# The last head's prompt state leaves the mixer and is multiplied in the routing pause, from copies in DRAM

## The chip, the cores and the metric

The kernel runs on one core of a Trainium2 chip. The metric is the device time of one execution in microseconds; the median of the timed runs counts. TensorE is called PE below, VectorE DVE, ScalarE ACT, GpSimd POOL and SyncE SP.

## What is computed

One layer of a hybrid decoder over 272 prompt positions (16 learned ones and 256 given) and 8 sampled tokens. A mixer (a projection of the normed input, a causal convolution of width 31 and a four-head retention) is followed by a mixture of 16 experts. Cut to what the change touches:

```python
def _retention_chunk(q, k, v, S, lg):
    ...
    k_dec = k * jnp.exp((L - 1.0 - idx)[:, None] * lg[None, :])[None, :, :, None]
    S_new = jnp.exp(L * lg)[None, :, None, None] * S + jnp.einsum('bjhd,bjhe->bhde', k_dec, v)
    return o, S_new
# mixer
y_a = jax.nn.silu(cn).astype(h.dtype) @ w_conv_out
y_b = (on * jax.nn.silu(g_ret.astype(jnp.float32))).astype(h.dtype) @ w_ret_out
out = (g_a * y_a + g_b * y_b) @ w_o
# experts, for t = the normed rows
eid = g_sel[:, None] * EXPERTS_PER_GROUP + idx
comb = p_g[:, None] * jnp.sum(w[..., None] * jax.nn.one_hot(eid, N_EXPERTS, dtype=jnp.float32), axis=1)
act = jax.nn.silu(hg) * hu * comb[:, :, None].astype(hg.dtype)
```

The prompt starts from a zero state, so each head's new prompt state is one product of its decayed keys (272 x 256) and its values (272 x 512), and it is only an output: nothing later in the layer reads it. The sampled tokens have states of their own, 32 of 256 x 512 (4 heads by 8 sequences), which are read, updated and written.

## The kernel before

**Mixer.** The projections and output products are 112 units (`UNITS`, numbered w); each makes 128 output features for up to 280 tokens, from 8 blocks of 128 inputs. Weights are float32 and every product is made in three passes: ACT makes the high part of a unit's weights (`hi`, w_hi), DVE the remainder (`lo`, w_lo), PE multiplies high by high, high by low and low by high (`passes`). Weights come in 1 MB chunks for two units each into three raw buffers. SP issues a load as soon as the last reader of its buffer (`lo`) is done. `hi` and `lo` of unit w + 2 are issued at the head of iteration w.

The retention runs beside the units, 22 steps from unit 37 (`STEP0`); k = w - STEP0. For each head h, step 4h has ACT and DVE write the decayed keys (k_tok, k_two), and step 4h + 4 makes the head's prompt state (tiles S, L1841 and L1842): for each of its two halves two float32 products of 512 columns and one single-pass one. ACT copies them to S_out (L920), and POOL stores them. The sampled states go through seven slots: POOL loads one, ACT scales it (`scaled`, L805), DVE adds the new outer product (L1323), PE multiplies by the queries (`samp_o`, L1788), POOL stores it; a slot's next load waits for the store to land. At the end of a head ACT copies the samples' sums out of their bank (osb, L948), and PE brings them to features one step later (tile ot, L1900). DMAs of states are on POOL's queue, weights on SP's.

The first unit of the convolution's output (cout) and of the last product (wo) read operands that ACT and DVE make one block after another; PE waits for each block with the semaphores clo_ready and mlo_ready.

**Routing pause.** After unit 111 PE brings the rows back to tokens (`to_tokens`). Then DVE chooses experts for every token in some forty small steps, while PE waits; four float32 products that nobody reads (`turn_over(4)`, L1756) stand in that wait. Then come the positions (tile pos), the rows of the first expert (tiles xp, L1959), the list of rows (idx, L1969) and the slot weights (tile ws, `weigh`, L1979).

**Experts.** 96 chunks of 1 MB are streamed through rings of four split chunks (`stream`, L2018: 12 products of 512 columns each); the name is g, u or d with the expert's number. On DVE the slot weights' copy (`slot_weights`, L1533) comes ahead of the remainders of chunks 2 and 3, of the tile Q (`last_slots`), which PE transposes in `last_places` behind chunks 0 and 1, and of what follows.

PE writes banks of PSUM in the order of the list `TILES`, seven in rotation; to open one it waits until the tile seven places ahead in the list was copied out.

## Time and profile before

| | us |
|---|---|
| median of 3 runs (lowest, highest) | 767.28 (767.08, 767.32) |
| the profiled execution's own time | 767.98 |
| its span | 766.2 |
| PE busy, DVE busy, ACT busy | 747.7, 667.9, 515.5 |

### The profile page before, as it was taken

The page shows a single profiled execution, that of the slowest core. Times are in us where ns is not written, and L with a number is a line of the kernel's source. Part 1 is how long each engine was busy: PE and PEld are TensorE (multiplying, and loading weights), DVE is VectorE, ACT ScalarE, POOL GpSimd, SP SyncE. Part 2 cuts the span into 40 slices and gives each one's busy share as a digit, 9 for nine tenths or more (in the row PEclk, how much of TensorE's full clock was granted, in tenths as well). Part 3 has the DMA queues.
Part 4 walks back from the last instruction along what each step waited for, and adds up shares of the span by engine and source line. Part 5 has one row for each costly group of instructions (what it writes and reads, how often), then busy time and mean ns, then how long its engine had stood idle before and what let it go on. Part 6 is the DMA issues. An engine that isn't in the chain of part 4 may idle for free.

```text
span 766.2 us, 12172 instructions
## 1 busy us (share of the span) xinstructions
PE 747.7 (98%) x4755; PEld 656.7 (86%) x4755; DVE 667.9 (87%) x917; ACT 515.5 (67%) x650; POOL 95.5 (12%) x119
## 2 busy tenths in 40 slices
PE   8999999999999999999999999999999999999994
PEld 5999999877777799999999978888888888888873
DVE  5699999888888887999979687988999899998897
ACT  6434446786868774335694465788888888888863
POOL 1100001224333400000020001011111111110000
PEclk9999999999999999999999999999999999999997
DMA  8945446698889954455458475899999999999972
GB/s 347 365 144 191 172 166 247 218 329 306 289 298 331 369 204 167 166 185 201 165 201 306 196 277 205 335 368 370 370 368 362 360 381 376 359 369 345 369 270 79
DMA packets 39030, 213.12 MB, mean 278 GB/s; under 512 B 7275, under 2 KB 7531, under 8 KB 19100
## 3 DMA queue, kind: packets, MB, share of 16 engines
q1 hardware_dynamic: 23268, 165.39, 58.3%
q0 software_dynamic: 15264, 45.55, 16.6%
q10 hardware_dynamic: 432, 1.31, 0.5%
q8 instruction: 40, 0.66, 0.3%
q14 instruction: 26, 0.21, 0.1%
HBM read 192.92 MB, written 31.65 MB: 293 GB/s over the span
## 4 chain that ended last, share of the span: by engine, by line
PE 58%; DVE 19%; DMA 13%; ACT 4%; issue 3%; POOL 1%; SPq 0%; DVEq 0%; ACTq 0%; POOLq 0%
PE bank L2018 34%; PE bank L1711 10%; DVE conv L1180 6%; DVE w_lo L1125 5%; PE bank L1714 5%; DMA out_ret_sample<-S_ring 5%; DMA out_ret_sample<-S_five 3%; DMA out_ret_sample<-xT 3%; DMA raw<-weights 3%; PE bank L2008 2%; ACT w_hi L776 1%; DMA xT<-in_state_ret 1%; PE bank L2050 1%; PE bank L1959 1%; DVE rot L1229 1%
## 5 line engine op out<-in xcount | busy, mean ns | idle before, releaser
L1130 DVE TENSOR_TENSOR ring_lo<-raw,ring_hi 128x2048 fp32r<-128x2048 f32 x72 | 163.5, 2288 | 22.5 <-ACT ring_hi L783 22.5
L1711 PE MATMUL bank<-h_hi,w_hi 128*128 128x264 f32 (+1 forms) x632 | 164.4, 292 | 0.3 <-ACT oT L941 0.3
L1711 PE MATMUL bank<-h_lo,w_hi 128*128 128x264 f32 (+1 forms) x632 | 161.4, 288 | 0.0
L1125 DVE TENSOR_TENSOR w_lo<-raw,w_hi 128x1024 fp32r<-128x1024 f32 x112 | 136.6, 1220 | 26.9 <-ACT w_hi L776 26.5
L776 ACT ACTIVATE w_hi<-raw 128x1024 fp32r<-128x1024 f32 x112 | 117.9, 1052 | 55.4 <-PE bank L1714 51.0
L783 ACT ACTIVATE ring_hi<-raw 128x2048 fp32r<-128x2048 f32 x72 | 138.2, 1919 | 20.0 <-PE bank L2018 19.1
L1711 PEld LDWEIGHTS bank<-h_hi,w_hi 128*128 128x128 f32 x632 | 119.1, 188 | 2.2 <-issue 1.5
L1711 PEld LDWEIGHTS bank<-h_lo,w_hi 128*128 128x128 f32 x632 | 119.1, 188 | 0.6
L1180 DVE SCALAR_TENSOR_TENSOR conv<-u,vec,conv 128x256 f32<-128x256 f32 x240 | 101.7, 477 | 0.6
L1714 PE MATMUL bank<-h_hi,w_lo 128*128 128x264 f32 (+1 forms) x632 | 92.3, 289 | 0.2 <-DVE w_lo L1125 0.2
L1714 PEld LDWEIGHTS bank<-h_hi,w_lo 128*128 128x128 f32 x632 | 84.5, 188 | 0.4 <-DVE w_lo L1125 0.4
L2018 PE MATMUL bank<-ring_hi,x_hi 128*128 128x512 f32 x192 | 76.2, 397 | 0.0
L2018 PE MATMUL bank<-ring_lo,x_hi 128*128 128x512 f32 x192 | 75.5, 393 | 0.0
L2018 PE MATMUL bank<-ring_hi,x_lo 128*128 128x512 f32 x192 | 75.5, 393 | 0.0
L1130 DVE TENSOR_TENSOR w_lo<-raw,w_hi 128x2048 fp32r<-128x2048 f32 x24 | 54.9, 2287 | 5.6 <-ACT w_hi L783 4.9
L783 ACT ACTIVATE w_hi<-raw 128x2048 fp32r<-128x2048 f32 x24 | 46.0, 1916 | 5.5 <-PE bank L2018 2.8
L2018 PEld LDWEIGHTS bank<-ring_lo,x_hi 128*128 128x128 f32 x192 | 36.5, 190 | 7.8
L2018 PEld LDWEIGHTS bank<-ring_hi,x_lo 128*128 128x128 f32 x192 | 36.4, 190 | 7.4
L2018 PEld LDWEIGHTS bank<-ring_hi,x_hi 128*128 128x128 f32 x192 | 36.4, 190 | 7.4
L733 POOL DMA_INDIRECT y_rows<-Y,idx x14 | 21.5, 1536 | 160.4 <-ACT Y L1087 160.4
L2018 PE MATMUL bank<-ring_hi,aT_lo 128*128 128x512 f32 x96 | 37.4, 389 | 0.0
L2018 PE MATMUL bank<-ring_lo,aT_hi 128*128 128x512 f32 x96 | 37.4, 389 | 0.0
(325 smaller groups left out, 1418.8 us busy)
## 6 DMA issues: line engine op xcount, KB each, us to landing
raw<-weights SPq DMA_DIRECT2D x152, 1024.0 KB, 7.0
S_ring<-in_state_ret POOLq DMA_DIRECT2D x20, 512.0 KB, 7.1
out_ret_sample<-S_ring POOLq DMA_DIRECT2D x20, 512.0 KB, 6.7
xT<-in_state_ret POOLq DMA_DIRECT2D x8, 512.0 KB, 6.9
out_ret_sample<-xT POOLq DMA_DIRECT2D x8, 512.0 KB, 7.3
S_five<-in_state_ret POOLq DMA_DIRECT2D x4, 512.0 KB, 5.4
out_ret_sample<-S_five POOLq DMA_DIRECT2D x4, 512.0 KB, 10.1
out_ret_prompt<-S_out POOLq DMA_DIRECT2D x8, 256.0 KB, 6.6
```

The costliest lines, as they stand in the source:

```text
L733: pool.indirect_dma_start(YD, bass.IndirectOffsetOnAxis(ap=idx[:, NE + e:NE + e + 1], axis=0), Y[:, e % 2, :], None, bounds_check=2 * N - ...
L776: act.activation(part_view(w_hi, w), raw_view(w), ACT.Copy).then_inc(hi_ready, 1)
L783: act.activation(ring_view(ring_hi, k), raw[raw_slot(c)][:, :].rearrange("p (k n) -> p k n", k=4), ACT.Copy).then_inc(chunk_hi, 1)
L1125: dve.tensor_tensor(part_view(w_lo, w), raw_view(w), part_view(w_hi, w).bitcast(f32), ALU.subtract).then_inc(lo_ready, 1)
L1130: dve.tensor_tensor(ring_view(ring_lo, k), raw[raw_slot(NCM + k)][:, :].rearrange("p (k n) -> p k n", k=4), ring_view(ring_hi, k).bitcast( ...
L1180: dve.scalar_tensor_tensor(out=out, in0=src, scalar=w_t, in1=out, op0=ALU.mult, op1=ALU.add).then_inc(conv_step, 1)
L1229: link(dve.tensor_tensor(rot[:, 1, :, cols], qk[:, p % 2, :, cols], sin2[:, :, cols], ALU.mult))
L1711: pe.matmul(out, hi[:, k, cols], b[:, k0 + k, :], start=first and k == 0 and j == 0, stop=False)
L1714: ins = pe.matmul(out, lo[:, k, cols], x_hi[:, k0 + k, :], start=False, stop=last and k == ks - 1)
L1959: ins = pe.matmul(b[:, f * 128:(f + 1) * 128], h2[0:nt, tt, at_f:at_f + 128], sel0[0:nt, tt, :], start=tt == 0 and f == 0, stop=tt == 2 an ...
L2008: ins = pe.transpose(b[:, f * 128:(f + 1) * 128], xg[:, e % 2, at_f:at_f + 128], ident)
L2018: ins = pe.matmul(out, a[:, kk, :], b[:, kk, :], start=first and kk == 0 and j == 0, stop=last and kk == 3 and j == 2)
```

## The change

- The state product of head 3 (`LATE`) is no longer made at step 16. Instead SP copies head 3's values and keys (v, v_two, k_tok, k_two: 512, 160, 256 and 80 KB) to DRAM (`late_to_dram`) ahead of weight chunk 29, and back into other places of SBUF (`late_back`) ahead of chunk 45. PE makes the same two products from them in the routing pause (`late_state`), ACT copies the result, SP stores it. The four products that nobody reads become one.
- The copies take the place, in SBUF, of the ring's fourth chunk, so ACT's split of chunk 3 waits for the stores. ACT and DVE wait for the copies to DRAM before they write over the sources.
- The other steps and the convolution's shares per unit stay where they were.
- `weigh(0)` is put between the two chunks of the first expert's g. Its bank is opened where it was. DVE's order is what it was.
- The first unit of cout and of wo takes the three passes of a block together, where before all low-weight passes stood at the end.

```diff
+LATE = NH - 1
@@ TILES
-            if 4 <= k <= 16 and k % 4 == 0:
+            if 4 <= k <= 16 and k % 4 == 0 and k // 4 - 1 != LATE:
                 for dt in range(2):
                     add((("S", k // 4 - 1, dt), "A"))
...
     add((("lg", 1), "D"))
+    for dt in range(2):
+        add((("S", LATE, dt), "A"))
@@ sync
+            def late_to_dram():
+                evacuated(sp, ("vt", 4 * LATE + 3))
+                sp.dma_start(V_SP, v_tok[LATE][:, 0:2, :]).then_inc(late_out, 16)
+                sp.wait_ge(vhi_ready, 2 * LATE + 2)
+                sp.wait_ge(vlo_ready, LATE + 1)
+                sp.dma_start(V2_SP, v_two[:, LATE % 2, :].bitcast(f32)).then_inc(late_out, 16)
+                evacuated(sp, ("kt", LATE, 0))
+                evacuated(sp, ("kt", LATE, 1))
+                sp.dma_start(K_SP, k_tok[:, :, :]).then_inc(late_out, 16)
+                sp.dma_start(K2_SP, k_two[:, :].bitcast(f32)).then_inc(late_out, 16)
+            def late_back():
+                seen(sp, ("m", FIRST["gate_b"] - 1))
+                sp.wait_ge(rows_stored, 16 * 3)
+                sp.wait_ge(late_out, 16 * 4)
...
             for c in range(NCM + RS + 2):
+                if c == (STEP0 + 14 + 7) // 2:
+                    late_to_dram()
+                if c == (FIRST["gate_b"] + 4 + 7) // 2:
+                    late_back()
                 load_weights(c)
...
+            for dt in range(2):
+                evacuated(sp, ("S", LATE, dt))
+                sp.dma_start(O["ret_prompt"][0, 0, LATE, dt * 128:(dt + 1) * 128, :], v_late[:, dt, :]).then_inc(late_stored, 16)
@@ scalar
+                if k == 3:
+                    act.wait_ge(late_stored, 16 * 2)
...
+            seen(act, ("S", LATE, 1))
+            for dt in range(2):
+                free(act.activation(v_late[:, dt, :], bank(("S", LATE, dt))[:, :], ACT.Copy))
@@ tensor, passes
+                if w in (FIRST["cout"], FIRST["wo"]):
+                    pe.wait_ge(lo_ready, w + 1)
+                    for k in range(ks):
+                        pe.wait_ge(clo_ready if w == FIRST["cout"] else mlo_ready, k + 1)
+                        for j, (a, b) in enumerate(((hi, x_hi), (hi, x_lo), (lo, x_hi))):
+                            ins = pe.matmul(out, a[:, k, cols], b[:, k, :], start=k == 0 and j == 0, stop=k == ks - 1 and j == 2)
+                    return ins
@@ tensor, pause
+            def late_state(dt):
+                pe.wait_ge(late_in, 16 * 4)
+                b = opened(("S", LATE, dt))
+                for tt in range(2):
+                    pe.matmul(b[:, :], k_late[:, tt, dt * 128:(dt + 1) * 128], v_late[:, tt, :], start=tt == 0, stop=False)
+                done(pe.matmul(b[:, :], k_late_two[:, dt * 128:(dt + 1) * 128], v_late_two[:, :], start=False, stop=True))
             to_tokens(1)
-            turn_over(4)
+            late_state(0)
+            late_state(1)
+            turn_over(1)
@@ tensor, experts
-                weigh(rd)
+                slots = opened(("ws", rd))
                 if rd:
+                    weigh(rd, slots)
...
                             if i == 1 and e == 0 and not rd:
+                                weigh(rd, slots)
                                 evacuated(pe, ("xp", e, 1, rd))
```

On SP's queue, from the first weight loads to the stores of the normed rows (raw<-weights is a weight chunk, h_rows<-h the rows), this stood before:

```order
L607 DMA x_tok<-tokens 128x1024
L619 DMA raw<-weights 128x2048 x63
L624 DMA h_rows<-h 128x1024 x2
L624 DMA h_rows<-h 8x1024
L619 DMA raw<-weights 128x2048 x89
```

and this stands there now:

```order
L630 DMA raw<-weights 128x2048 x29
L634 DMA v_later<-v 128x1024
L637 DMA v_two_later<-v_two 80x512
L640 DMA k_later<-k_tok 128x512
L641 DMA k_two_later<-k_two 80x256
L630 DMA raw<-weights 128x2048 x16
L648 DMA v_late<-v_later 128x1024
L649 DMA k_late<-k_later 128x512
...
L630 DMA raw<-weights 128x2048 x18
L661 DMA h_rows<-h 128x1024 x2
L661 DMA h_rows<-h 8x1024
L664 DMA out_ret_prompt<-v_late 128x512 x2
```

Ten DMAs are new on SP: four copies out behind chunk 28, four back behind chunk 44, and head 3's two stores, which were on POOL's queue.

On PE, from the router's products (wrg, xT) through the routing pause to the first expert's g chunks (ring_hi, x_hi), this stood before (L1756 is `turn_over`, VW the slot weights):

```order
L1773 MATMUL bank<-wrg,xT 8x20 x4
L1756 MATMUL bank<-con 128x512 x4
L1944 MATMUL bank<-member,count_r 128x16 x3
L1944 MATMUL bank<-member,count_r 8x16 x3
L1946 MATMUL bank<-member,count_r 128x16 x3
L1756 MATMUL bank<-con 128x512
L1959 MATMUL bank<-Q,h 128x128 x12
L1969 MATMUL bank<-V_,A_ 128x32 x6
L1979 MATMUL bank<-VW,A_ 128x32 x6
L2018 MATMUL bank<-ring_hi,x_hi 128x512
```

and this now:

```order
L1823 MATMUL bank<-wrg,xT 8x20 x4
L1989 MATMUL bank<-v_late,k_late 128x512 x2
L1990 MATMUL bank<-v_late_two,k_late_two 128x512
...
L1806 MATMUL bank<-con 128x512
L2004 MATMUL bank<-member,count_r 128x16 x3
...
L2019 MATMUL bank<-Q,h 128x128 x12
L2029 MATMUL bank<-V_,A_ 128x32 x6
...
L2077 MATMUL bank<-ring_hi,x_hi 128x512
L2077 MATMUL bank<-ring_hi,x_lo 128x512
L2077 MATMUL bank<-ring_lo,x_hi 128x512
L2038 MATMUL bank<-VW,A_ 128x32 x6
```

The two state products (the pair of rows L1989 and L1990 stands twice) replace three of the four unread ones, and the slot weights' six products have moved behind the twelve of the first g chunk.

At the end of cout's first unit PE had this before (c_hi and c_lo are the convolution's blocks):

```order
L1711 MATMUL bank<-c_lo,w_hi 128x264
L1711 MATMUL bank<-c_hi,w_hi 128x264
L1711 MATMUL bank<-c_lo,w_hi 128x264
L1714 MATMUL bank<-c_hi,w_lo 128x264 x8
L1711 MATMUL bank<-c_hi,w_hi 128x264
```

and has this now:

```order
L1757 MATMUL bank<-c_hi,w_lo 128x264
L1757 MATMUL bank<-c_hi,w_hi 128x264
L1757 MATMUL bank<-c_lo,w_hi 128x264
L1757 MATMUL bank<-c_hi,w_lo 128x264
L1761 MATMUL bank<-c_hi,w_hi 128x264
```

Behind the last block's two high-weight passes eight low-weight ones stood; now one does. The first unit of wo reads the same with m_hi and m_lo.

## Rows read from the trace of the kernel before

**Rows 1.** The page's busy times, whole span

```profile
PE 747.7 (98%) x4755; PEld 656.7 (86%) x4755; DVE 667.9 (87%) x917; ACT 515.5 (67%) x650; POOL 95.5 (12%) x119
```

**Rows 2.** The chain that ended last: start, length, what

```profile
233.55 7.70 DMA xT<-in_state_ret
...
241.27 1.06 ACT xT L805
...
258.61 1.72 PE bank L1841 x4
260.32 0.24 PE bank L1842
...
262.51 0.97 PE bank L1788 x8
263.49 2.17 PE bank L1711 x16
...
266.64 0.79 PE bank L1900 x8
...
486.18 16.38 PE bank L2018 x72
```

**Rows 3.** ACT's timeline: start, length, instruction [idle before, releaser]

```profile
256.81 1.06 ACT L805 ACTIVATE S_ring<-S_ring 128x1024 f32<-128x1024 f32 x1 [1.09 <-DMA S_ring<-in_state_ret]
257.88 1.28 ACT L966 ACT_TABLE_LOAD   x1
...
262.83 1.08 ACT L920 ACTIVATE S_out<-bank 128x512 f32<-128x512 f32 x2
263.78 2.38 ACT L948 ACTIVATE osb<-bank 8x512 f32<-8x512 f32 x4
```

**Rows 4.** Busy time by stretch; the last three: clock, DMA share, GB/s

```profile
240.00:250.00 10.00, 9.65 (x67) 7.30 (x64) 9.37 (x16) 6.68 (x12) 3.56 (x5) 1.00 0.89 299
250.00:260.00 10.00, 10.00 (x66) 7.85 (x64) 8.54 (x15) 7.04 (x10) 4.66 (x8) 1.00 1.02 413
```

**Rows 5.** PE's timeline in the first units of cout and wo

```profile
396.40 0.39 PE L1711 MATMUL bank<-c_hi,w_hi 128*128 128x264 f32 x1 [1.42 <-DVE c_lo L1380]
...
397.09 1.13 PE L1714 MATMUL bank<-c_hi,w_lo 128*128 128x264 f32 x8
...
421.10 0.39 PE L1711 MATMUL bank<-m_hi,w_hi 128*128 128x264 f32 x1 [0.65 <-DVE m_lo L1210]
```

**Rows 6.** PE's timeline from the routing pause on

```profile
450.14 3.70 PE L1756 MATMUL bank<-con 128*128 128x512 f32 x8
454.46 0.65 PE L1944 MATMUL bank<-member,count_r 128*128 128x16 f32 x6 [0.62 <-DVE member L1462]
...
463.35 1.52 PE L1979 MATMUL bank<-VW,A_ 128*128 128x32 f32 x12
...
471.87 1.06 PE L1989 MATMUL bank<-con,Q 128*128 128x128 f32 x6
```

**Rows 7.** DVE's timeline from the slot weights to Q

```profile
464.91 0.19 DVE L1533 COPY wslot<-bank 128x32 f32<-128x32 f32 x1
465.83 2.29 DVE L1130 TENSOR_TENSOR w_lo<-raw,w_hi 128x2048 fp32r<-128x2048 f32 x1 [0.72 <-issue]
468.04 2.28 DVE L1130 TENSOR_TENSOR ring_lo<-raw,ring_hi 128x2048 fp32r<-128x2048 f32 x1
470.24 0.95 DVE L1550 TENSOR_TENSOR Q<-mcon,pl 128x768 f32<-128x768 f32 x1
```

**Rows 8.** Busy time by stretch, columns as in rows 4

```profile
464.00:466.00 2.00, 2.00 (x12) 1.70 (x12) 1.06 (x3) 1.85 (x2) 0.56 (x1) 0.73 0.51 121
466.00:468.00 2.00, 2.00 (x6) 1.61 (x5) 2.00 (x1) 0.00 (x0) 0.00 (x0) 0.50 0.37 141
468.00:470.00 2.00, 2.00 (x9) 1.61 (x9) 2.00 (x2) 0.61 (x1) 0.00 (x0) 0.92 0.45 78
...
755.00:766.00 11.00, 0.82 (x4) 0.34 (x2) 7.21 (x12) 4.72 (x11) 0.00 (x0) 0.66 0.28 104
```

More of the change, by code:

```diff
@@ L323, with build @@
     _last[SLOT[_w]] = _w
-def build(nc, A, W, L, H2, YD, C, C2, O):
+def build(nc, A, W, L, H2, YD, LATER, C, C2, O):
     f32, f32r = mybir.dt.float32, mybir.dt.float32r
@@ L432, in build @@
             h2 = me.enter_context(nc.sbuf_tensor("h2", [128, 3, D], f32))
+        with ExitStack() as me:
+            me.enter_context(nc.sbuf_tensor("over_late", [128, 2 * hs // 4], f32))
+            v_late = me.enter_context(nc.sbuf_tensor("v_late", [128, 2, DV], f32))
+            k_late = me.enter_context(nc.sbuf_tensor("k_late", [128, 2, DK], f32))
+            v_late_two = me.enter_context(nc.sbuf_tensor("v_late_two", [80, DV], f32r))
+            k_late_two = me.enter_context(nc.sbuf_tensor("k_late_two", [80, DK], f32r))
+        V_SP, K_SP, V2_SP, K2_SP = LATER
         YY_CHUNKS = (NCE - 5, NCE - 4, NCE - 3)
@@ L482, in build @@
         Sp_stored = [sem(f"Sp_stored{i}") for i in range(2)]
+        late_out, late_in, late_stored = sem("late_out"), sem("late_in"), sem("late_stored")
         rows_stored, y_stored = sem("rows_stored"), sem("y_stored")
@@ L619, in load_weights @@
                 sp.dma_start(raw[raw_slot(c)][:, :], src).then_inc(raw_in[raw_slot(c)], 16)
+            def late_to_dram():
[12 more added lines that the diff above has]
+                sp.wait_ge(late_out, 16 * 4)
+                sp.dma_start(v_late[:, :, :], V_SP).then_inc(late_in, 16)
+                sp.dma_start(k_late[:, :, :], K_SP).then_inc(late_in, 16)
+                sp.dma_start(v_late_two[:, :].bitcast(f32), V2_SP).then_inc(late_in, 16)
+                sp.dma_start(k_late_two[:, :].bitcast(f32), K2_SP).then_inc(late_in, 16)
             for c in range(NCM + RS + 2):
+                if c == (STEP0 + 14 + 7) // 2:
+                    late_to_dram()
+                if c == (FIRST["gate_b"] + 4 + 7) // 2:
+                    late_back()
                 load_weights(c)
@@ L655, in _ @@
             for i in range(2):
-                sp.wait_ge(Sp_stored[i], 16 * NH)
+                sp.wait_ge(Sp_stored[i], 16 * (NH - 1))
+            sp.wait_ge(late_stored, 16 * 2)
         @block.gpsimd
@@ L697, in _ @@
                     load(n - 1 + SLOTS)
-            store_prompt(NH - 1)
             for i in (5, 6):
@@ L849, in _ @@
                     if f == 7:
-                        seen(act, ("S", NH - 1, 1))
+                        act.wait_ge(late_out, 16 * 4)
                     if f == 8:
@@ L913, in _ @@
                         scaled(2 * k + 1)
-                    if 4 <= k <= 16 and k % 4 == 0:
+                    if 4 <= k <= 16 and k % 4 == 0 and k // 4 - 1 != LATE:
                         h = k // 4 - 1
@@ L969, in _ @@
                         if q == 0:
-                            act.wait_ge(Sp_stored[0], 16 * NH)
-                            act.wait_ge(Sp_stored[1], 16 * NH)
+                            act.wait_ge(Sp_stored[0], 16 * (NH - 1))
+                            act.wait_ge(Sp_stored[1], 16 * (NH - 1))
                         seen(act, ("ut", q))
@@ L1213, in _ @@
                     dve.wait_ge(yhi_ready, f + 1)
+                    if f == 5:
+                        dve.wait_ge(late_out, 16 * 4)
                     dve.tensor_tensor(on_lo[:, f, OUT], oT[:, f, OUT], on_hi[:, f, OUT].bitcast(f32), ALU.subtract).then_inc(ylo_ready, 1)
@@ L1704, in passes @@
                 cols = slice(0, 128) if m is None else slice(m * 128, (m + 1) * 128)
+                if w in (FIRST["cout"], FIRST["wo"]):
[5 more added lines that the diff above has]
+                    return ins
                 for k in range(ks):
-                    if w == FIRST["cout"]:
-                        pe.wait_ge(clo_ready, k + 1)
-                    if w == FIRST["wo"]:
-                        pe.wait_ge(mlo_ready, k + 1)
                     for j, b in enumerate((x_hi, x_lo)):
@@ L1831, in _ @@
                     k = w - STEP0
-                    if 4 <= k <= 16 and k % 4 == 0:
+                    if 4 <= k <= 16 and k % 4 == 0 and k // 4 - 1 != LATE:
                         h = k // 4 - 1
@@ L1971, in find, with weigh @@
                 done(ins)
-            def weigh(rd):
+            def weigh(rd, b):
                 pe.wait_ge(vw_ready, 1)
-                b = opened(("ws", rd))
                 for c in range(2):
@@ L2129 @@
     YD = nc.dram_tensor("y_rows", (2 * N, D), _mybir.dt.float32).ap()
-    build(nc, A, W, L, H2, YD, C, C2, O)
+    LATER = (nc.dram_tensor("v_later", (128, 2, DV), _mybir.dt.float32).ap(), nc.dram_tensor("k_later", (128, 2, DK), _mybir.dt.float32).ap(),
+             nc.dram_tensor("v_two_later", (80, DV), _mybir.dt.float32).ap(), nc.dram_tensor("k_two_later", (80, DK), _mybir.dt.float32).ap())
+    build(nc, A, W, L, H2, YD, LATER, C, C2, O)
     r = _run(nc, [arrays], core_ids=[0])
```

## Prediction

> **What bounds the kernel now.** I read the page first, then the chain of work that ended last, then the timelines at the places that the change touches. PE is busy for 98% of the span [rows 1], and from 242 us on the chain consists mostly of PE's own work, one instruction behind the other [rows 2]. So work taken from PE is worth its length only up to the next thing that PE must wait for, and each place has to be read for what stands just behind it. Three such places matter.
>
> The first is the end of the retention. Up to 241 us the chain runs through the transfers of the sampled states: a load of 7.70 us, then ACT's scaling at 241.27, and only then PE [rows 2]. The last state's load is late as well: ACT idles 1.09 us for it and scales at 256.81. From there ACT works without a break: a table load, and at the end the two copies of the prompt state (262.83, 1.08 us) and the copies of the samples' sums, which end at 263.78 + 2.38 = 266.16 [rows 3]. PE needs those sums for the tile ot, which stands in the chain at 266.64 [rows 2]. ACT is thus some 0.4 us from being the bound there.
>
> The second is the first unit of cout and of wo, where PE idles 1.42 and 0.65 us for the last blocks of DVE [rows 5]. The third is the routing pause. PE idles only 0.62 us there beyond the unread products, until DVE has the choice at 454.46 [rows 6]. Behind the slot weights PE is dense until the tile Q is transposed at 471.87. DVE ends Q at 470.24 + 0.95 = 471.19, having worked without a break since 465.83 [rows 7]. DVE is 0.7 us ahead of PE there, no more. In the experts PE is dense: 72 products take 16.38 us, 0.2275 us each [rows 2], and a loss ahead of them is not made good.
>
> **The state product, out of the mixer.** It is four float32 products and two single-pass ones, 2 x (1.72 + 0.24) = 3.92 us of PE from 258.61 on [rows 2]. If PE alone decided, all of it would be gained. But behind it stand the samples' products (0.97 us), a unit from 263.49 on, and then the tile ot, which waits for ACT's copies. ACT's chain from 256.81 loses only the two copies, 1.08 us (less an overlap of 0.1): it ends at 265.1 where it ended at 266.16. The tile ot then starts at some 265.25 in place of 266.5, so the gain is 1.2 us, and 2.7 of the 3.92 us turn into a wait of PE before ot.
>
> **The copies to DRAM.** They are 1008 KB on SP's queue, 1.03 MB. SP can issue them once head 3's keys and values are split, at about 233 to 237 us, behind the weights of chunk 28, so they move at about 240 to 245. From 250 to 260 the DMA engines are fully busy at 413 GB/s, and from 240 to 250 they are busy 0.89 of the time [rows 4]. At 390 GB/s, between the two stretches' rates while busy (299 / 0.89 = 336 and 413), 1.03 MB take 2.65 us. The idle share of 240 to 250 can hide 1.1 us and, with the edges, I take 1.35; the other 1.3 us push the last state's load, for which ACT already waits. The bounds are 0 (SP's copies get in only where POOL's queue is idle) and 2.65. So this stretch nets -1.2 + 1.3 = +0.1 us, between -1.2 and +1.45. On the way back the copies are read in a stretch with half-idle engines, behind which weights are three chunks ahead: 0.
> The Trainium skill speaks against the copies too (page "Trainium Kernel Development and Optimization", section "Key Constraints"): DMAs issued from SP, ACT and POOL all run on the same 16 engines and interleave. A separate queue for the copies would then protect nothing, which is my reading of the full stretch; were it wrong, this stretch would give -1.2.
>
> **The two reordered units.** In cout, behind the last block's arrival at about 396.75, the eight low-weight passes from 397.09 on are 1.13 us by their record, some 0.98 without the overlap, 0.122 each [rows 5]. Seven of them move into the wait ahead, 7 x 0.122 = 0.85 us. But wo's first unit is released by DVE's last block at 421.10 whatever PE did before: DVE is itself dense up to it. The gain of cout is therefore spent as a longer wait before wo, and wo's own 0.85 us is what stays: -0.87 with the pass that is spared a restart. The bounds are 0 (none) and -1.7 (both).
>
> **The routing pause.** The new work is 3.92 + one unread product. The four unread ones take 3.70 us by record, 3.44 from start to start, so one is 0.86 and the new sum 4.78. From 450.2 it ends at 454.98, and the positions could start at 454.46 [rows 6]: +0.5 us, as DVE's next steps wait for them. ACT's two copies fit into its idle time before the first rows, and the stores of 512 KB have about 6 us until ACT's split of chunk 3, at 463.95 before, with idle DMA engines: 0. If they took longer than that, the price would appear one for one on ACT, and DVE's remainder of chunk 3 at 468.04 would be next.
>
> **The slot weights.** This edit moves no work, but it moves who waits. DVE's copy of the slot weights starts at 464.91, just as PE ends them (463.35 + 1.52), and stands ahead of the remainders of chunks 2 and 3 and of Q. From that copy to the end of Q are 471.19 - 464.91 = 6.28 us [rows 7]. Behind the change PE makes the first chunk's 12 products before them: 12 x 0.2275 = 2.73 us. So Q ends 2.73 us later, at 473.92 on the old scale, and PE starts its transpose at 474.0 where it did at 471.87 [rows 6]: +2.1 us. PE has nothing else to do then; it is through with both chunks at 463.42 + 2.73 + 1.46 + 2.73 = 470.3 and idles 3.7 us. Ahead of the change the same stretch of PE was slow for another reason (next part), which DVE's chain hid, so nothing is regained.
>
> **The clock.** After the thin products PE's granted clock was half (1.2 in place of 2.4 GHz): 0.73, 0.50 and 0.92 in three stretches of 2 us make 3.4 us at half clock from 464.9 to 468.3 [rows 8], a loss of 1.7 us of PE's work. At the end of the kernel, where PE is idle, it is 0.66. An idle time of 3.7 us in front of Q should bring such a phase, with dense products behind it that nothing hides: +1.5 us, from 0 to 1.7.
> The Trainium skill agrees in kind (page "TensorE: Matmul & The Clock Gate", section "Why this matters for your kernels"): gaps between bursts of products let the clock fall to half. By that rule this cost is there whenever the wait before Q is; by the trace it is likely.
>
> **The sum.** +0.1 - 0.87 + 0.5 + 2.1 + 1.5 = +3.3 us. On the profiled execution's own time, 767.98 (span 766.2, 1.78 around it), that is 771.3. That execution is 0.7 us above the median of the runs, so against the median of 767.28 I forecast **770.6 us**, 0.43% slower. A measurement of this kernel tells about 0.2%, 1.5 us, from no change.
>
> **Rivals.**
> - *PE decides everywhere, and the mixer pays in full* (12%). The 3.92 us would be gained if ACT could reach its copies earlier than its rows suggest. Then 767.28 - 3.92 - 0.87 + 0.5 + 2.1 = 765.1, faster. For it: the chain from 258.61 to 266.64 is all PE. Against it: ACT's end at 266.16. It decides if PE's ot starts before 264.5 on the old scale.
> - *The wait before Q is there, but the clock holds and the copies are hidden* (14%): 767.28 - 1.2 - 0.87 + 0.5 + 2.1 = 767.8, no difference that can be told. For it: the pause and the first chunk are denser than before.
> - *The copies cost in full, and the half clock falls on the first chunk and again behind the wait* (8%): +1.45 - 0.87 + 0.5 + 2.1 + 1.7 for one phase, and up to 1.7 for the other, which here delays the slot weights too: 773.9.
> - *All new work is hidden, with no wait before Q* (4%): only if DVE's split of chunk 2 got ahead of the slot weights' copy, which its order excludes: 763.7.
>
> The forecast's own case has 62%, from 769 to 772.6. The range to hold 8 in 10 takes in the second rival and ends below the third: 767.4 to 772.8. Faster by over 0.2% has 0.14 (first and fourth, less a part that ends within), within 0.2% 0.14, slower 0.72.
>
> **What the changed profile would show.** Right: idle time of PE of 1 to 3 us before ot, released by ACT's osb; ACT's wait for the last state's load longer than 1.09 us; PE's waits in cout and wo moved ahead, with three products behind the last block; no wait of PE for member; a wait of over 3 us for Q, and a granted clock near 0.5 behind it. The prediction is wrong if PE does not idle for Q, if ot moves forward by 3 us or more, or if ACT's split of chunk 3 waits for the stores (then it is worse).

## The result, and the profile after

| | before | changed |
|---|---|---|
| median (lowest, highest), us | 767.09 (766.41, 768.42), 14 runs | 769.37 (767.99, 773.92), 14 runs |
| ratio, 95% interval | | 1.0036 [1.0026, 1.0046] |
| profiled execution, its span | 767.98, 766.2 | 771.79, 770.0 |

The change makes the kernel 0.36% slower, some 2.8 us (the medians are 2.3 apart); 3.3 were forecast. It also makes it uneven: the runs of before lie within 2 us, those of the changed kernel within 6. Late runs of before exist too, but are few: of 35 more, timed beside e5 to e9, three are above 768, up to 770.10. The profiled execution of the changed kernel is the second longest of its 14, and its mean granted clock, 0.988, is the lowest (the 14 range to 0.994), so it shows more half clock than most runs had. The same kernel timed again gave 769.15 (767.78 to 774.88, 11 runs), 1.0031 [1.0015, 1.0046].

PE's waits in the changed kernel, as the view of waits lists them, longest sum first (sum, times, longest, us). They answer to [rows 5, 6]:

```profile
PE bank L2048 <- DVE Q L1597: 3.5, 1, 3.5
...
PE bank L1950 <- ACT osb L990: 0.9, 1, 0.9
PE bank L1757 <- DVE c_lo L1427: 0.6, 1, 0.6
PE bank L1757 <- DVE m_lo L1255: 0.5, 1, 0.5
```

The wait for c_lo has gone from 1.42 to 0.6, that for member is gone, and two are new: 0.9 before ot (L1950) and 3.5 before Q is transposed (L2048). PE's timeline shows the pause and the wait for Q:

```profile
448.72 1.98 PE L1989 MATMUL bank<-v_late,k_late 128*128 128x512 f32 x4
450.14 0.80 PE L1990 MATMUL bank<-v_late_two,k_late_two 80*128 80x512 f32 x1
450.78 1.88 PE L1989 MATMUL bank<-v_late,k_late 128*128 128x512 f32 x4
452.10 0.80 PE L1990 MATMUL bank<-v_late_two,k_late_two 80*128 80x512 f32 x1
...
465.23 1.42 PE L2038 MATMUL bank<-VW,A_ 128*128 128x32 f32 x12
...
473.03 1.71 PE L2048 MATMUL bank<-con,Q 128*128 128x128 f32 x6 [3.53 <-DVE Q L1597]
```

DVE's timeline tells why Q is late; it answers to [rows 7]:

```profile
466.69 0.19 DVE L1580 COPY wslot<-bank 128x32 f32<-128x32 f32 x1 [2.88 <-PE bank L2038]
467.61 2.29 DVE L1175 TENSOR_TENSOR w_lo<-raw,w_hi 128x2048 fp32r<-128x2048 f32 x1 [0.72 <-ACT ring_hi L825]
469.82 2.28 DVE L1175 TENSOR_TENSOR ring_lo<-raw,ring_hi 128x2048 fp32r<-128x2048 f32 x1
472.02 0.95 DVE L1597 TENSOR_TENSOR Q<-mcon,pl 128x768 f32<-128x768 f32 x1
```

DVE stands idle for 2.88 us in front of a copy of 0.19 us, and the 6.28 us from that copy to the end of Q are the same as before. What the clock does behind the wait, by stretches (the column before the last two is the granted clock), columns as in rows 4:

```profile
468.00:470.00 2.00, 1.50 (x7) 0.90 (x5) 2.00 (x2) 0.46 (x1) 0.00 (x0) 1.00 0.00 0
470.00:472.00 2.00, 0.00 (x0) 0.00 (x0) 2.00 (x1) 0.23 (x1) 0.00 (x0) 0.90 0.43 94
472.00:474.00 2.00, 0.97 (x4) 0.62 (x5) 2.00 (x3) 0.00 (x0) 0.00 (x0) 0.50 1.03 422
474.00:476.00 2.00, 2.00 (x9) 1.65 (x10) 1.85 (x3) 0.18 (x1) 0.00 (x0) 0.50 1.00 356
476.00:478.00 2.00, 2.00 (x7) 1.71 (x7) 1.38 (x2) 1.74 (x3) 0.59 (x1) 0.50 0.98 397
478.00:480.00 2.00, 2.00 (x9) 1.63 (x9) 0.89 (x1) 1.08 (x1) 0.40 (x1) 0.89 0.91 313
```

The clock falls at 471.6, while PE still idles, and is at 1.2 GHz until 478.4 (0.90 and 0.89 of 2 us are 0.4 us each at half, with 6 us between them): 6.8 us, twice the phase of [rows 8], and PE has work in the last 5.4 of them. The length is not fixed. In the second profile of the same kernel (e9), where PE waits for Q until 477.00, the phase behind a wait of 3.52 us is 3.4 us long:

```profile
476.00:478.00 2.00, 1.00 (x6) 0.64 (x6) 2.00 (x3) 0.00 (x0) 0.00 (x0) 0.95 1.04 438
478.00:480.00 2.00, 2.00 (x10) 1.98 (x11) 1.95 (x4) 0.60 (x1) 0.00 (x0) 0.50 0.97 406
480.00:482.00 2.00, 2.00 (x8) 1.57 (x7) 1.26 (x2) 1.90 (x2) 0.99 (x1) 0.69 1.02 377
```

In the mixer there is a second such phase, behind the new wait for ot. ACT's and PE's timelines there, and the clock by stretches:

```profile
255.97 1.06 ACT L847 ACTIVATE S_ring<-S_ring 128x1024 f32<-128x1024 f32 x1 [0.81 <-DMA S_ring<-in_state_ret]
...
261.99 2.38 ACT L990 ACTIVATE osb<-bank 8x512 f32<-8x512 f32 x4
```

```profile
264.42 1.06 PE L1950 MATMUL bank<-con,osb 128*128 128x8 f32 x8 [0.95 <-ACT osb L990]
```

```profile
266.00:268.00 2.00, 2.00 (x14) 2.00 (x13) 2.00 (x5) 1.67 (x5) 0.00 (x0) 0.70 0.86 323
268.00:270.00 2.00, 2.00 (x10) 1.91 (x9) 1.68 (x3) 0.40 (x2) 0.00 (x0) 0.50 0.76 311
270.00:272.00 2.00, 2.00 (x11) 1.76 (x10) 0.61 (x2) 0.26 (x1) 0.00 (x0) 0.94 0.74 233
```

Worked out in the same way, this phase is 3.4 us long. It begins at 266.8, 2.4 us after the wait has ended, while PE is at work.

To compare kernels, the table below gives PE's start times at fixed places of their profiled executions, and stretches between them. "ot" is the tile of [rows 2] at 266.64, whose first product starts at 266.48 before; "gate" is the sum of squares that follows it; "cout" and "wo" are those units' first products, "rows home" the first transpose behind wo, "weights" the first product of what follows the first expert's rows, "Q" its transpose, "down" the first transpose of the first expert's features.

| kernel | ot | ot to gate | cout to wo | wo to rows home | weights to Q | Q to down | span |
|---|---|---|---|---|---|---|---|
| before | 266.48 | 8.53 | 25.23 | 15.57 | 8.52 | 12.83 | 766.2 |
| changed | 264.42 | 10.19 | 24.38 | 15.40 | 10.65 | 15.23 | 770.0 |
| changed, second profile | 268.91 | 10.19 | 24.36 | 14.90 | 10.66 | 14.44 | 773.1 |
| products back (e1) | 264.34 | 8.69 | 24.38 | 14.90 | 7.89 | 12.92 | 762.6 |
| products moved alone (e2) | 265.90 | 8.53 | 25.19 | 15.67 | 10.65 | 15.69 | 770.6 |
| two units alone (e3) | 265.75 | 8.53 | 24.36 | 14.90 | 8.54 | 12.83 | 763.9 |
| wait filled (e4) | 268.35 | 8.68 | 24.36 | 15.26 | 10.64 | 12.89 | 769.5 |
| copies alone (e5) | 265.83 | 8.53 | 25.18 | 15.46 | 8.54 | 12.84 | 765.4 |
| state alone (e6) | 263.85 | 8.67 | 25.20 | 15.14 | 7.90 | 12.89 | 763.3 |
| cout alone (e7) | 266.17 | 8.52 | 24.38 | 15.75 | 8.52 | 12.83 | 765.3 |
| slot copy behind Q (e8) | 264.14 | 8.68 | 24.37 | 14.91 | 7.08 | 12.89 | 761.6 |
| the same, no copies out (e10) | 265.27 | 10.18 | 24.39 | 15.57 | 7.07 | 12.90 | 765.0 |
| the same again (e12) | 263.40 | 8.74 | 24.37 | 15.90 | 7.07 | 12.89 | 762.0 |
| units, products, slot copy (e11) | 266.09 | 8.53 | 24.37 | 14.92 | 7.08 | 12.89 | 762.9 |

### The profile page after: what moved, and what is told of

The parts are those of the page before. It is cut to its first block, busy times and chain, and to the rows that moved or that the text cites. A ratio compares the mean times of both kernels' runs of the same rounds, so it can differ in the third digit from the quotient of the medians.

```text
span 770.0 us, 12172 instructions
## 1 busy us (share of the span) xinstructions
PE 748.5 (97%) x4749; PEld 657.8 (85%) x4749; DVE 668.2 (87%) x917; ACT 515.3 (67%) x650; POOL 94.7 (12%) x117
## 4 chain that ended last, share of the span: by engine, by line
PE 55%; DVE 19%; DMA 15%; ACT 5%; issue 4%; POOL 1%; DVEq 0%; ACTq 0%; POOLq 0%
PE bank L2077 34%; PE bank L1761 9%; DMA out_ret_sample<-S_ring 7%; DVE conv L1225 6%; DVE w_lo L1170 5%; PE bank L1764 5%; DMA out_ret_sample<-xT 3%; DMA out_ret_sample<-S_five 2%; PE bank L2067 2%; DMA raw<-weights 1%; ACT w_hi L816 1%; DMA S_ring<-in_state_ret 1%; PE bank L2111 1%; PE bank L2019 1%; DVE ring_lo L1175 1%
## 5 line engine op out<-in xcount | busy, mean ns | idle before, releaser
L2077 PE MATMUL bank<-ring_hi,aT_hi 128*128 128x512 f32 x96 | 37.3, 389 | 0.0
```

Source lines behind the costliest of these rows:

```text
L2077: ins = pe.matmul(out, a[:, kk, :], b[:, kk, :], start=first and kk == 0 and j == 0, stop=last and kk == 3 and j == 2)
```

## Experiments

The theory was the prediction's: the slot weights' new place makes Q late (2.1) and drops the clock (1.5), the units give 0.87, and the mixer nets nothing. The rivals: the copies to DRAM are the cost; the clock falls for another reason than the wait.

### Which part costs: the slot-weight products

**e1, the products back ahead of the first chunk**, all else as changed:

```diff
-                            if i == 1 and e == 0 and not rd:
-                                weigh(rd, slots)
```
(and `weigh` again behind the first expert's rows.)

> The changed kernel with the slot weights' products back ahead of the first expert's g chunks; state product, copies and the two units as changed. Theory A (the slot weights' place costs 2.1 us of waiting before Q and 2.4 us of half clock behind it): no wait of PE before Q, 766.1 us, 1.0 us faster than before and 3.3 faster than the changed kernel, since at the first rows of the pause the changed kernel was 0.97 us ahead. Theory B (the copies, the state product in the pause or its stores cost the time): as the changed kernel, 769.4 us.

764.94 (763.83 to 770.26, 12 runs), 0.9985 [0.9970, 0.9999]. That is 0.5% from the changed kernel's 1.0036, so the products' place costs 3.9 us (uncertain by 1.4; the stretches of the two profiles give 2.76 + 2.31 = 5.1). The clock stays at 1.00 through the pause, and of the wait for Q 0.8 is left:

```profile
PE bank L1950 <- ACT osb L990: 1.3, 1, 1.3
...
PE bank L2048 <- DVE Q L1597: 0.8, 1, 0.8
```

"Weights to Q" is 7.89, less than the 8.52 of before, although the order there is the same: before had half clock on the first chunk, and this kernel, with the state product in the pause, has not. e6 shows the same (7.90). The prediction had no term for it.

**e2, the kernel before with only the products moved.**

> The kernel before with only the slot weights' products moved between the two g chunks. Theory A: PE idles 3 to 3.7 us before Q, the clock is half behind it, 767.1 + 2.1 + 2.4 = 771.6 us (range 769.5 to 772). Theory B: 767.1 us, no change. A third theory, that the wait alone counts and not the clock, gives 769.2.

771.49 (770.63 to 772.99, 6 runs), 1.0059 [1.0045, 1.0074]: 4.5 us for one line moved, without any of the rest. The wait is the same:

```profile
PE bank L2036 <- DVE Q L1583: 3.5, 1, 3.5
```

In the table, 2.13 us stand in "weights to Q" and 2.86 in "Q to down".

**e4, the wait filled**: four unread products (`turn_over(4)`) ahead of the transpose of Q in the changed kernel.

> The changed kernel with four float32 products of 512 columns that nobody reads (3.44 us) put on PE between the g chunks and Q's transpose, where it idles 3.5 us. Theory A (idle time there brings the half clock, which costs 2.4 us on top of the wait): the granted clock stays at 1.00, the transpose starts no earlier, 769.4 - 2.4 = 767.0 us, and the runs scatter less. Rival (the half clock comes from the thin slot-weight products or at random): the clock falls all the same, 769.4 us or more.

771.01 (768.71 to 771.40, 6 runs), 1.0043 [1.0028, 1.0059]: not faster, where 767.0 was expected. Locally the theory holds: Q starts as late as in the changed kernel (10.64), the clock stays at 1.00, and "Q to down" is 12.89 instead of 15.23. But in this execution ot starts at 268.35, 3.9 us later than in the changed kernel's first profile, ahead of anything that the edit touches. ACT scales the last sampled state at 259.90, behind a wait of 2.29 for it, where the changed kernel did at 255.97, so it is late by as much. The clock was half once more in the mixer as well (0.97, 0.50 and 0.68 from 242 to 248, 3.4 us). The local reading stands; the total is a miss that a late stream of states explains for the profiled run, and which wasn't shown for the other five.

**e8, one line of DVE moved.** TensorE's order stays that of the change; DVE makes Q first and copies the slot weights behind it:

```diff
             x_part(0, 1, 0)
-            slot_weights(0)
...
                             last_slots()
+                            slot_weights(0)
```

> The changed kernel with one line of VectorE moved: the copy of the slot weights stands behind the making of Q instead of ahead of the two long low-part products, so that VectorE doesn't wait for TensorE's slot-weight products before it makes Q. TensorE's order is that of the change. Theory A (VectorE's wait of 2.88 us for that copy makes Q late, TensorE idles 3.5 us before Q, and the idle time brings the half clock behind it): no wait for Q over 1 us, clock held behind Q, and 764 to 765.5, as the version that has the products back in their old place. Rival B (Q is late for another reason, or the clock falls from the thin stretch ahead and not from this wait): 769 with the wait or the half clock still there.

765.74 (763.15 to 768.86, 12 runs), 0.9990 [0.9972, 1.0007], against 1.0031 [1.0015, 1.0046] of the changed kernel on the same chip, where its profile has again a wait and half clock. DVE's timeline:

```profile
461.74 2.29 DVE L1175 TENSOR_TENSOR w_lo<-raw,w_hi 128x2048 fp32r<-128x2048 f32 x1 [0.23 <-issue]
463.95 2.28 DVE L1175 TENSOR_TENSOR ring_lo<-raw,ring_hi 128x2048 fp32r<-128x2048 f32 x1
466.15 0.95 DVE L1596 TENSOR_TENSOR Q<-mcon,pl 128x768 f32<-128x768 f32 x1
467.02 0.18 DVE L1580 COPY wslot<-bank 128x32 f32<-128x32 f32 x1
```

DVE no longer stops, PE transposes Q at 467.16 without a wait, and "weights to Q" is 7.08, PE's own work alone. So the order on DVE, not the products' place on PE, was what cost. Against the changed kernel the ratios give 3.1 us (uncertain by 1.8), the stretches of the profiles 5.1 to 5.9; with e1's 3.9 and 5.1 this suggests that most runs lose less to the clock than the profiled ones did. Total and highest runs are above the expected 764 to 765.5; the profiled run is the second fastest (763.39), so the mixer's scatter may be why, but no profile shows it.

### The two units

**e3, the kernel before with only the two units reordered**, and **e7, with only cout's.** Against the changed kernel both have the state product and the slot weights where they were before, without copies; e7's further edit keeps the old order for wo:

```diff
-                if w in (FIRST["cout"], FIRST["wo"]):
+                if w in (FIRST["cout"],):
```

> The kernel before with only the first unit of cout and of wo in the new order of passes. Theory A (cout's gain is spent in wo's wait, one of two 0.85 us stays): 766.2 us. Rival 1, both stay: 765.4. Rival 2, DVE or DMA is the bound behind both: 767.1, no change.

> The kernel before with one unit in the new order, that of cout. The prediction had cout's 0.85 us spent in a longer wait of wo for m_lo, so that nothing of it is left: then 766.7 and a wait of 1.5 us before wo. If the 0.85 stays: 765.8, with wo's wait as before (0.65).

e3: 765.71 (765.07 to 766.03, 12 runs), 0.9982 [0.9974, 0.9991], 1.4 us faster, between the first two expectations. e7: 766.73 (766.31 to 767.74, 11 runs), 0.9999 [0.9990, 1.0008], which is the time expected if cout's gain is spent. "cout to wo" falls by the 0.85 in every kernel that has the new order. "wo to rows home" ranges from 14.90 to 15.90, also between kernels with the same order of passes, because a weight chunk ahead of wo lands early in some executions and late in others. ACT's timeline of before shows where the wait begins (wo's last operand block is due at 421.1):

```profile
413.68 1.06 ACT L776 ACTIVATE w_hi<-raw 128x1024 fp32r<-128x1024 f32 x1 [1.65 <-DMA raw<-weights]
```

and DVE's of before what it makes of it:

```profile
414.77 1.23 DVE L1125 TENSOR_TENSOR w_lo<-raw,w_hi 128x1024 fp32r<-128x1024 f32 x1 [0.57 <-ACT w_hi L776]
```

A weight chunk lands late, ACT splits it late, and DVE stands for 0.57 us in the chain that ends in m_lo. In e3 the same chunk lands earlier:

```profile
412.15 1.06 ACT L807 ACTIVATE w_hi<-raw 128x1024 fp32r<-128x1024 f32 x1 [0.89 <-DMA raw<-weights]
```

and DVE has no idle time from 403 to 418. In e12 DVE stands 0.91 us for the chunk, the wait for m_lo is 1.00, and the stretch is the longest, 15.90. Where both units are reordered the stretch follows this idle time: 14.90 to 14.92 with none (e1, e3, e8, e9, e11), 15.26 with 0.26 (e4), 15.40 with 0.40 (changed), 15.57 with 0.58 (e10), 15.90 with 0.91.

So kernels have to be compared at the same lateness of the chunk. From cout's first product to rows home (the sum of the two stretches):

| DVE's idle time for the chunk | both units old | only cout new | both units new |
|---|---|---|---|
| 0.57, 0.58 | 40.80 (before) | | 39.96 (e10) |
| 0.41, 0.40 | 40.64 (e5) | | 39.78 (changed) |
| none | 40.34 (e6) | 40.13 (e7) | 39.26 (e3) |

Both units together are worth 0.84, 0.86 and 1.08. cout alone is worth 0.21: most of its 0.85 comes back as a longer wait for m_lo, 0.83 us where e6 has 0.20 (not the expected 1.5, as the chunk was early here). From PE's restart behind c_lo to its restart behind m_lo pass 24.70 and 24.72 in the first row, 24.55 and 24.55 in the second, 24.26 and 24.06 (e6, e7) in the third: DVE and its chunk set wo's release, with cout in either order.

### The mixer and the copies

**e5, the kernel before with the copies out and back, which nobody reads.**

> The kernel before with one addition: the two pieces of v and k of the last head that the moved product would use are copied out to DRAM early and back in the pieces of the gate, and nothing reads them; the state product of the last head stays in the mixer, and the two units and the slot-weight products keep their old order. Theory A (the copies share the DMA engines with the stream of the states in the mixer, as the page of the changed kernel suggests, where GpSimd's queue fell from about 98 to between 50 and 69 per cent of the engines in 239 to 245 us): 0.5 to 1.5 us slower than before (767.2 to 768.2), scattered more from run to run, with the waits of ScalarE for the states' load longer than before in the mixer. Rival B (the copies lie in gaps of the stream): 766.7, within 0.3 of before, waits as before.

766.37 (766.10 to 767.56, 11 runs), 0.9993 [0.9983, 1.0004]. The copies alone cost nothing, and do not scatter these times. They do share the engines. The view of DMA for 239 to 245 (queue: packets, MB, share of the 16 engines), before (an execution with a late stream, see below):

```profile
q0 software_dynamic: 511, 1.83, 82.2%
q1 hardware_dynamic: 9, 0.04, 1.7%
```

and with the copies (e5):

```profile
q0 software_dynamic: 425, 1.56, 63.7%
q1 hardware_dynamic: 389, 0.87, 38.1%
```

The states' queue (q0) gives way by a quarter of its share (the expectation's "about 98" is before's first half of this time, 96.6% in 239 to 242). This is the sharing that the Trainium skill states (page "Trainium Kernel Development and Optimization", section "Key Constraints"); the trace agrees, but sharing alone set no price. With the copies the last state is scaled at 256.16, behind a wait of 1.29, and PE still reaches ot at 265.83 without a wait: with the state product in the mixer PE arrives there no earlier, and the product covers this delay.

**e6, the state product moved, with its copies, the other edits undone.**

> The changed kernel with the two units and the slot-weight products in their old order: only the last head's state product is moved, with its copies. Theory A (the moved product takes 1.2 to 2 us out of the mixer, its copies give about 1 back there, and it costs 0.44 in the pause): 766 to 767, within 0.5 of before. Rival B (the whole product of 3.92 us comes off the mixer, less 0.44 in the pause): 763.2. Rival C (copies at their full 2.65 us): 768.5. Between the first output-cast wait and the pieces of cout the anchors tell them apart.

766.07 (765.11 to 771.12, 12 runs), 1.0003 [0.9985, 1.0022]. The sum is as expected, but not its make: the lowest seven lie between 765.1 and 766.2, the other five between 768.0 and 771.1. Of what its profile gains on that of before, 0.62 is not the mixer's but the first chunk's full clock ("weights to Q", 7.90 against 8.52).

**e9, the changed kernel again**, for a second profile.

> The changed kernel again beside the others on the same chip: 769.4 (1.0036 of before). If the extra half-clock stretch behind the first output-cast wait in the mixer belongs to the kernel and not to the one profiled execution, it is there again; if the mixer's times vary from execution to execution with the stream of the states, its anchors there differ from those of the first profile by 1 us or more.

That profile fell on its slowest run (774.88). ACT's timeline in the mixer:

```profile
242.00 1.06 ACT L847 ACTIVATE xT<-xT 128x1024 f32<-128x1024 f32 x1 [2.14 <-DMA xT<-in_state_ret]
...
246.74 1.06 ACT L847 ACTIVATE S_ring<-S_ring 128x1024 f32<-128x1024 f32 x1 [2.50 <-DMA S_ring<-in_state_ret]
...
260.47 1.06 ACT L847 ACTIVATE S_ring<-S_ring 128x1024 f32<-128x1024 f32 x1 [2.35 <-DMA S_ring<-in_state_ret]
```

The last state comes 4.5 us later than in the first profile (255.97), and ot at 268.91, behind a PE wait of 1.71, 4.49 us later too. The phase at half clock behind ot is there again (10.19), that behind Q is shorter (14.44 against 15.23).

**e10 and e12, no copies out.** As e8, but the moved product multiplies other data of the same size: 768 KB are read back from the input states, and 240 KB are copied out some hundred us earlier. The last head's prompt state is thereby not the reference's.

```diff
-                sp.dma_start(v_late[:, :, :], V_SP).then_inc(late_in, 16)
+                sp.dma_start(v_late[:, :, :], A["state_ret"][0, 0, 0].rearrange("(t p) e -> p t e", p=128)).then_inc(late_in, 16)
```

> As the version with the slot-weight copy behind Q, but nothing is copied out to DRAM in the mixer: the moved product multiplies other data of the same size (768 KB read from the input states, 240 KB copied out some hundred us earlier), so the last head's prompt state is not the reference's. The loads back, the product and every order stay. Theory A (the copies out are what makes the stream of the states late in some executions, once the product no longer covers it): 763.2 to 764 in nearly all executions, no group at 767 to 769. Rival B (the product's absence alone lays the stream's own lateness open): median about 765.7 with the same two groups as with the copies. Rival C (the copies cost a steady part too): the mixer's last ot wait and what follows begin 0.5 us or more earlier than 264.1 also in the fastest executions.

> The version without the copies out again (other data of the same size in the moved product, so the last head's prompt state is not the reference's), for more executions: the first six lay between 762.8 and 766.8, where the same version with its copies had five of twelve at 767.4 or above. Theory A (the copies out bring the group at 767 to 769): none of some twelve executions above 767.3, median 763.5 to 764.5. Rival B (the product's absence lays it open by itself): again a third or more of them above 767.

764.24 (762.79 to 766.79, 6 runs), 0.9961 [0.9946, 0.9976], and 763.75 (762.97 to 763.94, 5 runs), 0.9953 [0.9940, 0.9967]. Against e8's 0.9990 the copies cost 2.2 to 2.8 us in the mean, with intervals of over 1 us on either side, while the fastest runs differ by only 0.36 (762.79 and 763.15). Late executions are a large part of it: of e8's twelve runs four are at 767.4 or more (the expectation above counts five, one too many), of these eleven none; with so few runs on different chips the counts alone prove little. The stream can be late without them too: the first profile of this version, its slowest run, has a wait of 1.80 us for a state and ot at 265.27. In the second nothing of ACT's waits for a state is left:

```profile
254.96 1.05 ACT L849 ACTIVATE S_ring<-S_ring 128x1024 f32<-128x1024 f32 x1
...
260.97 2.37 ACT L992 ACTIVATE osb<-bank 8x512 f32<-8x512 f32 x4
```

and ot starts at 263.40, with no wait listed.

Taken together the profiles say more than each alone. A late stream is late well ahead of the copies. POOL issues the load into the slot S_five between 220.82 and 223.83 in ten profiles, and at 225.01 or later in four: e9, e10, e4 and before (227.05). The changed kernel's two profiles:

```profile
223.01 0.72 POOL L710 DMA_DIRECT2D S_five<-in_state_ret  x1 [6.00 <-DMA out_ret_sample<-S_five]
```

```profile
225.01 0.72 POOL L710 DMA_DIRECT2D S_five<-in_state_ret  x1 [5.95 <-DMA out_ret_sample<-S_five]
```

SP issues its first copy at 232.25 in the second. Neither the missing product (258 us) nor the copies out have run by 225 us (only e10 and e12 have copied their 240 KB, and of these two one is on time). What the copies do is make the last state later, and far more so in a late stream:

| the stream at 225 us | last state scaled, without the copies out | with them |
|---|---|---|
| on time | 254.70 to 255.81 (e2, e3, e7, e11, e12) | 255.40 to 256.16 (changed, e1, e5, e6, e8) |
| late | 256.81, 256.82 (before, e10) | 259.90, 260.47 (e4, e9) |

That is 0.8 us in the mean of the one row, whose two groups overlap a little, and 3.1 to 3.7 in the other. In all eight profiles with the product moved ot starts 8.44 or 8.45 us behind the start of that scaling.

### A version that beats both

**e11**: the kernel before with the two units reordered, the products in their new place, and DVE's copy behind Q; without the moved state product and its copies.

> A candidate to beat both: the kernel before with the two units reordered, the slot-weight products behind the first three features' product and VectorE's slot-weight copy behind Q, and without the moved state product and its copies. Theory A (the stay of the product keeps the mixer steady; the two units give 1.3; the products' new place no longer delays Q): 764.5 to 765.7, narrow from run to run. Rival B (with the pause left thin the clock falls before Q, so that the products' new place gives nothing): 765.7. Rival C (the wait for Q returns): 769 or more.

764.65 (764.46 to 767.92, 12 runs), 0.9977 [0.9967, 0.9986]: 1.8 us faster than before and 4.5 than the change, with nine of its twelve runs within 0.5 us. By stretches at the place of [rows 8] (columns as there):

```profile
464.00:466.00 2.00, 2.00 (x17) 1.88 (x16) 2.00 (x2) 1.39 (x1) 0.00 (x0) 1.00 0.39 145
466.00:468.00 2.00, 2.00 (x10) 1.61 (x9) 2.00 (x2) 0.52 (x1) 0.00 (x0) 1.00 0.73 193
```

Where before had 0.73 and 0.50, the clock is full. The thin products now have the chunk's dense ones ahead of them, which is argued to be the reason; the thin products in their old place do not bring the half clock by themselves, since e1 and e6 have them there and keep the full clock. The stretch to Q is 1.44 us shorter. That part of the change was worth having once DVE's order was put right. The difference to e8 is the moved state product with its copies: by the two ratios it costs 1.0 us on top, which their intervals do not tell from none, and the spread (763.15 to 768.86).

## Why the prediction was right

The time, 769.37, is within its range and 1.2 us from 770.6, and the place of the cost is the predicted one, the wait for Q with the half clock behind it. That the sum comes so near is in part luck, since errors of the mixer's terms cancel. The sum by its terms:

| term | predicted | measured | from |
|---|---|---|---|
| mixer and copies | +0.1 | +0.4 (-1.0 to +1.9) | e6's ratio, less the pause, plus the first chunk's 0.62 |
| of it the product | -1.2 | -1.7 to -2.3; -1.2 with a late stream, -2.7 with an early one | ratios of e10 and e12 against e11, less the pause; ot, e10 against before, e12 against e11 |
| of it the copies | +1.3 | +2.2 to +2.8, uncertain by 1.8; 0.8 on time, 3.1 to 3.7 late | ratios of e8 against e10, e12; last state scaled |
| two units | -0.87 | -1.4 (-2.0 to -0.7); -0.84 to -1.08 | e3's ratio; profiles at the same lateness of the chunk |
| pause | +0.5 | +0.45 | 6.56 - 6.40 and 2.41 - 2.12, stretches around pos |
| Q late | +2.1 | +2.13 | weights to Q |
| clock behind Q | +1.5 | +2.4 and +1.6 (changed, two profiles), +2.9 (e2) | Q to down |

With e3's ratio the measured terms sum to +4.0, or +3.2 with the clock of the changed kernel's second profile; the ratio says 2.8 (2.0 to 3.5).

Of the signs that were named, two did not come: PE's wait before ot was 0.95, just under the 1 to 3, and ACT's wait for the last state was 0.81, not over 1.09. And the first rival's sign came, by a hair: ot started at 264.42, before 264.5. It was not that rival, though, because PE waited there for osb in seven of the eight profiles with the product moved, so PE did not decide alone.

**The slot weights**: right in mechanism and size. 2.73 us more work of PE ahead of DVE's copy became 2.88 us of DVE's idle time, and 2.13 before Q. Its step "nothing is regained" holds only while that copy stands where it does: e8 and e11 gain 1.4 there.

**The clock**: right in kind, and the bound too small. "From 0 to 1.7" took the length of the phase, 3.4 us, from the one phase in [rows 8]. In e9 it was 3.4 us behind the wait too and cost 1.6, near the 1.5 of the sum; in the changed kernel's first profile and in e2 it lasted 6.8 us and cost 2.4 and 2.9, and the bound didn't hold. The third rival had "up to 1.7 for the other", a second phase, which came too, though not where it was put: behind ot, 1.5 us (10.19 against 8.68). The Trainium skill's rule (page "TensorE: Matmul & The Clock Gate", section "Why this matters for your kernels"), that gaps between bursts let the clock fall, is given there for long gaps. For Q's 3.5 us the trace agrees each time (changed, e2, e9), and with the wait filled (e4) no phase came. On waits as short as those before ot that section says nothing, and the profiles do not decide: 0.95 (changed), 1.24 (e10) and 1.71 us (e9) had the phase behind them, 0.67 (e6), 0.97 (e8), 1.3 (e1) and 1.7 (e4) had not.

**The state product**: the net was right because two sizes were off in opposite directions. The chain itself was right to the hundredths: from a scaling at 256.81 it puts ot at 265.25, and e10, whose last state is scaled at 256.82, has ot at 265.27. But "ACT's chain from 256.81 loses only the two copies" took the start of that chain as given. It is the landing of the last state that sets it, and that moves between executions: 254.96 in e12, 256.81 before, 260.47 in e9. The profile of before was an execution with a late stream. With an early one, PE is dense up to ot with the product (266.09 in e11, no wait), and taking the product away gives 2.7.

**The copies**: "the other 1.3 us push the last state's load" is right as a mean but wrong as a steady price. Alone they cost 0 (e5). On time, they delay the last state by some 0.8 us, which shows only once the product is gone; in a stream that is already late at 225 us they make it 3.1 to 3.7 us later, more than the product's 2.7 us could cover. That the copies do this is read from the four groups of profiles, not from a single copy seen to delay a state. Why the stream is late by 225 us in some executions stays open. So does why none of e5's eleven runs was late, which the product's cover alone does not explain.

**The two units**: right in size and in mechanism. The step "wo's first unit is released by DVE's last block at 421.10 whatever PE did before" holds: at the same lateness of the chunk the release comes equally long behind c_lo within 0.02 us, without the idle time within 0.2, and cout alone is worth 0.21 of its 0.85 (e7). Its reason, "DVE is itself dense up to it", is wrong: DVE stood 0.57 us for a late weight chunk six microseconds earlier, and 0.49 for ACT's m_hi just ahead of the last block. That idle time varies from none to 0.91 us between executions and moves the stretch behind wo by up to 1.0, for which the prediction had no term. In the changed kernel's own profile, against that of before, the two give 0.85 + 0.17.

**The pause**: right. The wait for member is gone, and ACT's split of chunk 3 did not wait for the stores: they were issued at 456.0 and 456.5 and landed 2.4 to 2.7 us later, and the split at 462.98 follows ACT's instruction before it without a wait.

## What to carry to other kernels

When an edit makes one engine's instruction later, look at the reader's queue: a reader of 0.2 us that stands ahead of long work holds all of it back, and moving that reader can turn the same edit from a loss into a gain. A wait on the engine that bounds can cost a stretch of half clock on top of the delay itself, here 1.6 to 2.9 us on top of 2.1; price both. Work that stands in front of a late input is also cover for a stream that is sometimes late: if taking it away makes the times scatter, compare distributions, and not one profile, before keeping the edit. And compare stretches only between executions in which the same input came equally late: against the profile of before, cout alone seems worth 0.67 us (40.80 less 40.13), against one whose chunk was as early, 0.21.

## What the runs showed of the hardware

The half-clock phase around and behind a wait of 3.5 us was 6.8 us long in two profiles and 3.4 in a third, and 3.4 us behind one of 0.95. Waits of 0.67 to 1.72 us before ot were followed by it in three of seven profiles, and not in the order of their length. A phase of 3.4 us also came with no idle time of PE in the ten us ahead of it, behind the thin products of before (from 464.9). What else decides was not found. One MB of copies beside a state stream that held 82.2% of the engines took a quarter of that stream's share (63.7% left). The last state came some 0.8 us later with them where the stream was on time, and 3.1 to 3.7 us later where it was late already; the first cost nothing as long as PE had work in hand.
